# A decoder layer in three-pass fp32r matmuls: the first two feed-forward matrices reordered over ScalarE, GpSimd and VectorE, and the right end of memory moved by 128 bytes

## The reference, cut to what matters

```python
x = x + g1 * (concat(rms(o_sb), rms(o_dsa)) @ w_o)          # output projection
h = rms(x) * norm2_gain * (1 + sc2) + sh2                   # modulated norm
x = x + g2 * ((silu(h @ w_gate) * (h @ w_up)) @ w_down)     # feed-forward, width 2816
return rms(x) * final_gain * (1 + sc_f) + sh_f              # sc_f, sh_f from w_mod_final
```

## Time and profile before

| what | before |
|---|---|
| median of 3 runs | 1518.36 us (1517.19 to 1519.18) |
| the profiled execution | 1517.11 us |
| its span | 1515.4 us |
| TensorE busy | 1338.2 us, 88% |
| VectorE busy | 1078.7 us, 71% |
| ScalarE busy | 731.6 us, 48% |
| GpSimd busy | 732.5 us, 48% |
| TensorE's mean granted clock, share of full | 0.945 |
| chain that ended last: TensorE, VectorE | 42%, 5% |

### The profile page before, as it was taken

One profiled execution on the slowest core, in us unless ns is written; L12 is line 12 of the kernel. 1 busy time (PEld: TensorE's weight loads), 2 busy tenths in 40 slices (PEclk: granted clock), 3 DMA queues, 4 the chain that ended last, 5 costly groups with the idle time before them and its releaser, 6 DMA issues.

```text
span 1515.4 us, 18608 instructions
## 1 busy us (share of the span) xinstructions
PE 1338.2 (88%) x6085; PEld 1076.1 (71%) x6085; DVE 1078.7 (71%) x1582; ACT 731.6 (48%) x1262; POOL 732.5 (48%) x674
## 2 busy tenths in 40 slices
PE   1779999995877788876998889999999999999997
PEld 1657888774666566654776668888888888888786
DVE  4857599997777777755375987666666666577787
ACT  4436677734777778765222623322333333354332
POOL 1163444553445448877000235555555556587552
PEclk9799899996889899997799999999999999999999
DMA  9670234455343133320572225444444446889532
GB/s 337 185 210 16 83 119 145 139 181 132 74 95 78 47 98 100 89 68 24 222 227 103 87 84 183 143 155 160 159 150 149 154 160 204 296 303 333 182 112 111
DMA packets 124395, 223.35 MB, mean 147 GB/s; under 512 B 9450, under 2 KB 52564, under 8 KB 124052
## 3 DMA queue, kind: packets, MB, share of 16 engines
q1 hardware_dynamic: 124308, 222.27, 44.7%
HBM read 160.90 MB, written 57.93 MB: 144 GB/s over the span
## 4 chain that ended last, share of the span: by engine, by line
PE 42%; DVE 5%; issue 2%; ACT 1%; DMA 1%; POOL 0%; DVEq 0%; POOLq 0%; ACTq 0%; SPq 0%
PE ps_out L2150 26%; PE ps_out L2176 12%; PE ps_out L1492 2%; PE ps_out L1508 1%; DVE mod_acc_final L1575 1%; DMA scr_mod_final<-mod_acc_final 1%; PE ps_out L1862 0%; DVE y_gated L1605 0%; ACT square_junk L2070 0%; DVE x L2420 0%; DMA wgu_raw<-in_w_gate_dram 0%; DVE down_part L2418 0%; DVE y_full L1593 0%; DVE xhat L1874 0%; PE ps_out L1524 0%
## 5 line engine op out<-in xcount | busy, mean ns | idle before, releaser
L1849 POOL TENSOR_TENSOR wgu_lo<-wgu_raw,wgu_hi 128x512 fp32r<-128x512 f32 x64 | 91.5, 1436 | 147.3 <-ACT wgu_hi L1841 147.3
L2086 POOL TENSOR_TENSOR dn_lo<-dn_raw,dn_hi 128x512 fp32r<-128x512 f32 x77 | 127.3, 1671 | 67.2 <-ACT dn_hi L1994 67.1
L1841 ACT ACTIVATE wgu_hi<-wgu_sum 128x512 fp32r<-128x512 f32 x88 | 55.3, 632 | 201.9 <-DVE wgu_sum L2240 77.8
L2150 PE MATMUL ps_out<-h_b_t_hi,wgu_hi 128*128 128x512 f32 x352 | 140.4, 399 | 3.9 <-ACT p_part L1976 2.9
L2150 PE MATMUL ps_out<-h_b_t_hi,wgu_lo 128*128 128x512 f32 x352 | 139.8, 397 | 0.0
L2150 PE MATMUL ps_out<-h_b_t_lo,wgu_hi 128*128 128x512 f32 x352 | 139.7, 397 | 0.0
L1994 ACT ACTIVATE dn_hi<-dn_raw 128x1024 fp32r<-128x1024 f32 x77 | 81.2, 1062 | 114.7 <-PE ps_out L2176 57.1
L1148 POOL TENSOR_TENSOR a_rows<-beta,stick_left 128x1024 f32<-128x1024 f32 (+3 forms) x64 | 77.1, 1207 | 109.5 <-DVE stick_left L1196 109.5
L413 POOL TENSOR_TENSOR win_lo<-win_raw,win_hi 128x256 fp32r<-128x256 f32 (+1 forms) x84 | 62.3, 774 | 133.9 <-ACT win_hi L404 133.9
L2176 PE MATMUL ps_out<-dn_hi 128*128 128x512 f32 x308 | 120.4, 391 | 0.0
L2176 PE MATMUL ps_out<-dn_hi,dn_lo 128*128 128x512 f32 x308 | 120.1, 390 | 0.0
(11 more groups left out here) (327 smaller groups left out, 3827.0 us busy)
## 6 DMA issues: line engine op xcount, KB each, us to landing
scr_act_sums<-act_sums SPq DMA_DIRECT2D x11, 1792.0 KB, 6.8
dn_raw<-scr_act_sums SPq DMA_DIRECT2D x77, 256.0 KB, 5.2
wgu_raw<-in_w_gate_dram SPq DMA_DIRECT2D x11, 1024.0 KB, 5.4
wgu_raw<-in_w_up_dram SPq DMA_DIRECT2D x11, 1024.0 KB, 5.4
wd_sums<-in_w_down_dram SPq DMA_DIRECT2D x11, 1024.0 KB, 5.0
scr_wd_sums<-wd_sums SPq DMA_DIRECT2D x11, 1024.0 KB, 4.1
dn_raw<-scr_wd_sums SPq DMA_DIRECT2D x44, 256.0 KB, 7.0
win_raw<-in_w_in_dram SPq DMA_DIRECT2D x20, 512.0 KB, 4.5
```

Source lines behind the costliest of these rows:

```text
L1849: pool.tensor_tensor(sl[slot(m, x)][:], src, sh[slot(m, x)][:].bitcast(F32), ALU.subtract).then_inc(wlp, 1)
L2086: pool.tensor_tensor(bl[q % NSLOT][:, 1], braw[entry(q)][:, 1], bh[q % NSLOT][:, 1].bitcast(F32), ALU.subtract).then_inc(dlw, 1)
L2150: last = pe.matmul(bank(m, b), a[s][:, t], h[x][t // 2][:, t % 2], start=(fresh and t == 0 and a is sh and h is hh), stop=(t == 3 and a is ...
```

## The change

`xhat` is split in two: blocks 0 to 3 stay with VectorE (`early_xhat`) and come in front of step 8's work, not behind it; blocks 4 to 7 go to ScalarE (`late_xhat`). The transposes T0 to T7 take places one step or half a step later, the modulations and the splits with them. `late_rstd` of block 6 comes in front of GpSimd's first low parts. The six low parts of S3, S4 and A22 of the first two matrices go from VectorE to GpSimd. The hand-written orders of ScalarE and VectorE change. `mod_acc_final` goes from the left to the right, into the first 2 KB of a tile that the first modulated block overwrites, so the first `modulate` waits for all four stores of it. The pad on the right grows from 32 to 160 bytes.

```diff
-    fa = sbuf(nc, ctx, "mod_acc_final", [P, HALF])
+    fa = nc.alloc_sbuf_tensor_at("mod_acc_final", [P, HALF], F32, offset=g.top - 16 * 1024)
...
-    STEP_T = {(0, 9): 0, (1, 10): 1, (0, 10): 2, (1, 11): 3, (0, 11): 4, (1, 12): 5, (0, 12): 6, (0, 13): 7}
-    AFTER_COPY = {11: (0, 1), 12: (2, 3), 13: (4, 5), 14: (6,), 15: (7,)}
+    STEP_T = {(1, 10): 0, (0, 10): 1, (1, 11): 2, (0, 11): 3, (1, 12): 4, (0, 12): 5, (1, 13): 6, (0, 13): 7}
+    AFTER_COPY = {11: (0,), 12: (1, 2), 13: (3, 4), 14: (5, 6), 15: (7,)}
...
         then.first_highs(act)
+        for i in range(4, 7):
+            then.late_xhat(act, i)
         squares(NT - 1)
...
         late_rstd(4, 6, 2)
+        late_rstd(6, 7, 3)
         then.first_lows(pool, 0)
-        late_rstd(6, 7, 3)
         then.first_lows(pool, 1)
...
+            if n == 8:
+                for x in range(4):
+                    then.early_xhat(dve, x)
             dve.wait_ge(ysc, n + 1)
...
-            if n == 8:
-                for x in range(4):
-                    then.xhat(dve, x)
-            if n in (10, 11, 12):
-                then.split(dve, n - 10)
+            if n in (11, 12, 13):
+                then.split(dve, n - 11)
...
     def low_by_vector(self, m, x):
-        return x in LOW_DVE or (m < 2 and x in (P_S3, P_S4, P_A22))
+        return x in LOW_DVE
...
     def modulate(act, n):
+        if n == 0:
+            act.wait_ge(p4.fmo, 64)
...
-        pe.wait_ge(xhd, 4 + 4 * h)
+        pe.wait_ge(xha if h else xhd, 4)
...
+    def early_xhat(dve, i):
+        dve.wait_ge(p4.rs2, 1)
+        dve.wait_ge(x1_out[0], 16 * 4)
+        dve.tensor_scalar(g.x1[:, i], g.x1[:, i], g.rstd2[:, i:i + 1], None, ALU.mult).then_inc(xhd, 1)
+
+    def late_xhat(act, i):
+        act.wait_ge(p4.rs2, {4: 2, 5: 2, 6: 3, 7: 4}[i])
+        if i == 4:
+            act.wait_ge(p4.ybm, p4.NY)
+        act.activation(xh[i // 2 - 2][:, i % 2], g.x1[:, i], ACT.Copy, scale=g.rstd2[:, i:i + 1]).then_inc(xha, 1)
...
         def await_prepared(m):
             sp.wait_ge(wlp, lows_pool(m, P_A22))
-            if m < 2:
-                sp.wait_ge(wld, lows_dve(m, P_A22))
             sp.wait_ge(sums, sums_through(m, P_S4))
...
         act.wait_ge(p4.fmd, p4.NF)
         copy_p1(0)
         w_hi(act, 0, P_S1)
+        w_hi(act, 1, P_S1)
+        late_xhat(act, 7)
         copy_p1(1)
-        for n in range(KD, KD + 4):
-            modulate(act, n)
-        w_hi(act, 1, P_S1)
-        for n in range(KD + 4, 2 * KD):
+        for n in range(KD, 2 * KD):
             modulate(act, n)
         w_hi(act, 0, P_S2)
         w_hi(act, 1, P_S2)
+        t_hi(P_S2, t2, 2)
+        w_hi(act, 0, P_S3)
+        w_hi(act, 1, P_S3)
+        silu(0, 0)
+        w_hi(act, 0, P_S4)
+        w_hi(act, 1, P_S4)
+        t_hi(P_S3, f_t3, 4)
         act.wait_ge(hfr, 2 * KD)
         t_hi(P_S4, f_b22, 0)
-        w_hi(act, 0, P_S3)
-        w_hi(act, 1, P_S3)
-        t_hi(P_S2, t2, 2)
-        silu(0, 0)
-        t_hi(P_S3, f_t3, 4)
-        w_hi(act, 0, P_S4)
-        w_hi(act, 1, P_S4)
-        t_hi(P_A22, f_t4, 6)
         w_hi(act, 0, P_A22)
         w_hi(act, 1, P_A22)
+        t_hi(P_A22, f_t4, 6)
         w_hi(act, 2, P_A11)
         silu(0, 3)
         w_hi(act, 2, P_S1)
...
             pool.tensor_tensor(bl[q % NSLOT][:, 1], braw[entry(q)][:, 1], bh[q % NSLOT][:, 1].bitcast(F32),
                                ALU.subtract).then_inc(dlw, 1)
 
+        for x in (P_S3, P_S4, P_A22):
+            for m in range(2):
+                w_lo_pool(pool, m, x)
         for m in range(2, MATS):
             w_lo_pool(pool, m, P_A11)
             w_lo_pool(pool, m, P_A12)
...
             dve.tensor_tensor(bl[q % NSLOT][:, 0], braw[entry(q)][:, 0], bh[q % NSLOT][:, 0].bitcast(F32),
                               ALU.subtract).then_inc(dla, 1)
 
-        for i in range(4, 7):
-            xhat(dve, i)
         w_sum(0, P_S1)
-        xhat(dve, 7)
         w_sum(1, P_S1)
         split(dve, P_A12, f_t4, 1, 8, 4)
         w_sum(0, P_S2)
         w_sum(1, P_S2)
+        w_lo(0, P_S1)
+        w_lo(1, P_S1)
+        w_sum(0, P_S3)
         for pc in range(2):
             t_sum(t1, f_t3, f_b11, pc, full=KD + 2 * pc + 2)
         for pc in range(2):
             dve.wait_ge(tsm, pc + 1)
             dve.tensor_copy(hh[P_S1][pc][:], t1[pc][:]).then_inc(hid, 1)
-        w_lo(0, P_S1)
         for pc in range(2):
             dve.wait_ge(hid, 5 + pc)
             dve.tensor_tensor(hl[P_S1][pc][:], t1[pc][:], hh[P_S1][pc][:].bitcast(F32), ALU.subtract).then_inc(lod, 1)
-        w_lo(1, P_S1)
-        w_sum(0, P_S3)
         w_sum(1, P_S3)
         for pc in range(2):
             t_sum(t2, f_b22, t1, pc, full=KD + 4 + 2 * pc + 2, before=pc + 1)
         w_sum(0, P_S4)
+        w_lo(0, P_S2)
+        for pc in range(2):
+            t_lo(P_S2, t2, pc, 1 + pc)
+        w_sum(1, P_S4)
+        w_lo(1, P_S2)
         for pc in range(2):
             t_sum(f_t3, f_b22, f_t3, pc)
-        w_sum(1, P_S4)
         for pc in range(2):
-            t_lo(P_S2, t2, pc, 3 + pc)
-        w_lo(0, P_S2)
-        w_lo(1, P_S2)
-        for pc in range(2):
-            t_lo(P_S3, f_t3, pc, 5 + pc)
-        w_lo(0, P_S3)
-        w_lo(1, P_S3)
+            t_lo(P_S3, f_t3, pc, 3 + pc)
         first_act(0)
-        for pc in range(2):
-            t_lo(P_S4, f_b22, pc, 1 + pc)
         u2_of(0)
         u4_of(0)
-        w_lo(0, P_S4)
+        for pc in range(2):
+            t_lo(P_S4, f_b22, pc, 5 + pc)
+        u2_of(1)
+        u4_of(1)
         for pc in range(2):
             t_sum(f_t4, f_t4, t2, pc, before=3 + pc)
-        u2_of(1)
-        u4_of(1)
-        w_lo(1, P_S4)
         finish(0, 3)
         for pc in range(2):
             t_lo(P_A22, f_t4, pc, 7 + pc)
-        w_lo(0, P_A22)
-        w_lo(1, P_A22)
         w_sum(2, P_S1)
         finish(1, 3)
         finish(0, 1)
...
-            co.enter_context(nc.sbuf_tensor("right_pad", [P, 8], F32, side="right"))
+            co.enter_context(nc.sbuf_tensor("right_pad", [P, 40], F32, side="right"))
```

More of the change, by code:

```diff
@@ L1733, in phase5 @@
     raw_loaded = k.sems("wgu_loaded", 2)
-    xhd = k.sem("xhat2_ready")
+    xhd = k.sem("xhat2_dve_ready")
+    xha = k.sem("xhat2_act_ready")
     tr = k.sem("x1_transposed")
@@ L1863, in transposes @@
         m.then_inc(tr, 1)
-    def xhat(dve, i):
-        dve.wait_ge(p4.rs2, (1, 2, 3, 4)[max(0, i // 2 - 1) + (i == 7)])
-        if i < 4:
-            dve.wait_ge(x1_out[0], 16 * 4)
-            dst = g.x1[:, i]
-        else:
-            if i == 4:
-                dve.wait_ge(p4.ybm, p4.NY)
-            dst = xh[i // 2 - 2][:, i % 2]
-        dve.tensor_scalar(dst, g.x1[:, i], g.rstd2[:, i:i + 1], None, ALU.mult).then_inc(xhd, 1)
+    def early_xhat(dve, i):
[7 more added lines that the diff above has]
+        act.activation(xh[i // 2 - 2][:, i % 2], g.x1[:, i], ACT.Copy, scale=g.rstd2[:, i:i + 1]).then_inc(xha, 1)
     def split(dve, x, f, pc, full, at_):
@@ L1930, in sync @@
         sp.wait_ge(x1_out[1], 16 * (NT // 2))
-        sp.wait_ge(xhd, NT)
+        sp.wait_ge(xha, 4)
         load_wd(0)
@@ L1982, in silu @@
                 if m == 0:
-                    act.wait_ge(xhd, NT)
+                    act.wait_ge(xha, 4)
             else:
@@ L2290, in first_act @@
                 dve.wait_ge(x1_out[1], 16 * (NT // 2))
-                dve.wait_ge(xhd, NT)
+                dve.wait_ge(xha, 4)
             dve.tensor_tensor(acts[:, S_A11], bank(m, X), sg[:, 0], ALU.mult).then_inc(mulr, 1)
@@ L2505, in phase5 @@
     then.first_raw, then.spill, then.modulate, then.first_highs = first_raw, spill, modulate, first_highs
-    then.first_lows, then.transposes, then.xhat, then.split = first_lows, transposes, xhat, early_split
+    then.first_lows, then.transposes, then.split = first_lows, transposes, early_split
+    then.early_xhat, then.late_xhat = early_xhat, late_xhat
     return Programs(sync, scalar, gpsimd, tensor, vector)
```

## The result

The changed kernel takes 1502.15 us, median of four runs (1498.33 to 1503.82), beside 1517.78 for the kernel before with its fourth run (1512.39 to 1519.18). The ratio of the changed kernel's times to the other's is 0.9902, with a 95% interval of 0.9882 to 0.9923: 15 us faster (12 to 18). The profiled execution took 1503.75 us with a span of 1502.0.

The account below looks back on a forecast made before the run. TensorE was taken to bound from 907 us on, VectorE in front of it. Reordering 5.5 plus pad 6.5 made 12.0 off 1517.1, so 1505.1; the median lies 1.25 higher: forecast 1506.5, range 1500 to 1514.5.

Parts of the forecast that it names:

- The case named most likely: Whole kernel: reordering gains 5.5 us and the pad 6.5, 12.0 in sum; chance 0.50.
- Part 6, the pad: Matmuls of twenty matrices: the pad aligns `high` tiles with `low` weights, 6.0 us, with the output projection 6.5 taken.
- my slower rival: A11, S1, A12, S3: the new offset lengthens matmuls by 0.0066 us, 1520.2 us in all; slower side 0.09.
- the rival "worth nothing": All matrices: the pad gains nothing, only the reordering's 5.5 us remains, 1512.9 us; chance 0.24.
- Part 1, the seam at T0: Output projection: early `xhat` removes T0's 4.67 us wait, T1 waits 2.65; gain 2.5 us, less 1.2 to 1.75 if the clock falls.
- Part 2, the late `xhat` on ScalarE: Before T8: the fourth `xhat` ends at 848.5, T8 starts at 848.6 and not 851.65, 3.0 us earlier.
- Part 3, six low parts to GpSimd: First two matrices: VectorE gives up 3.6 us but is held 6.6, so it loses 3 us.
- Part 4, the load: Matrix 2's weights: SP issues the load at 877.3, not 888.6, and VectorE's 5.00 us wait goes.
- Part 5, the chain: VectorE from last x (844.5) to `w_sum(2, S1)`: 43.9 us, reached at 888.4; TensorE restarts at 901.3, 5.8 us earlier.
- The reordering: All parts but the pad, in front of TensorE's restart: 5.5 us gained, bounds 0 and 10.

Follow-up runs that it names:

- The last version: Changed kernel with only A22's two low parts on GpSimd, and TensorE's transposes and ScalarE's modulations moved in two tables of places: 1494.16 us, ratio 0.9875.

## Why the prediction was right, and where not

1506.5 us with a range of 1500.0 to 1514.5 was predicted, faster with 0.86; it is 1502.15 and faster, by 15 us where 12 were forecast. The case named most likely is the one that came: both halves of the change work, and they add. By steps:

*Part 6, the pad: right in kind, too small.* Put at 6.0 us over twenty matrices, measured 8.6, and 8.7 in the whole time by the run with the pad alone. The mis-sized term is S2, S3 and S4. I took 0.0025 us a matmul for S2 and let S3 and S4 keep what they had; all went to 0.2267, which is 0.07, 0.06 and 0.05 us a product in place of 0.03, 0 and 0. A11, S1, A12 and A22 gave what I had put for them. S3 I could have had from my own rule: both its h parts are `high`, and my slower rival counts it with those. S4's tiles all lie on the left, and no address of its own changed; so "each `high` tile gets the same place as the weights it meets" is not the full rule. That the pad alone, without the order, gives 8.7 us refutes the rival "worth nothing" (0.24). The Trainium skill, "SBUF — State Buffer", section "Who interferes with whom", says that TensorE never waits on anyone for SBUF. The prediction read a price of 0 for the pad out of it, and the runs go against that price. In this kernel a matmul's spacing depends on the distance between the two ends of memory; whether other engines have a part in it no run shows. The sum of the slower rival has a slip: 48 and 24 matmuls at its steps make 7.5 us and not 7.3, which changes nothing.

*Part 1, the seam at T0.* The times came as worked out: T1's gap 2.89 (2.65 expected), T4's 1.18 (1.2), T6's 2.02 (2.1), each released by ScalarE's modulation. The clock did fall behind T1 (at 815.4), and A11 starts at 842.41, 1.4 us before the old time, which is what the 2.5 us less a fall of 1.2 would give. But 1.4 is partly luck, as the two executions lost the clock differently further in front; where they lost it alike it was 0.7. The part that I credited with it, the early place of `xhat`, is worth nothing by the run with it undone; the loss at T1 eats it.

*Part 2, the late `xhat` on ScalarE: wrong.* The step that failed is "the fourth ends at 848.5, T8 starts at 848.6". The last x was to be there at 844.5; it came at 847.1. Three low parts in a row on GpSimd, 4.70 us, stand right beside steps 14 and 15 and hold VectorE by 2.3 us in all. From the last x to T8 it then took 4.7 us and not 4.1. T8 came at 851.78, not a bit earlier than before. A11 to T8 even grew from 7.8 to 9.4 us. The last version, in which those low parts hold nothing, has 7.9 again. What the late `xhat` is worth by itself is not shown: no run moves it back.

*Part 3, six low parts to GpSimd.* "VectorE loses 3 us": the sign is right, the size 1.7 to 2.7 (with six back) or 2.0 to 3.0 for four of them. The holds are in the trace (1.79 and 1.60 us for 0.69). The Trainium skill, "SBUF — State Buffer", section "Who interferes with whom", says that a VectorE instruction with two SBUF inputs and a GpSimd instruction that reads SBUF are in each other's way. The trace agrees, by these two rows.

*Part 4, the load.* Issued at 879.28 (877.3 expected), no wait of VectorE left. It is worth 4.8 to 5.8 us in the stage by the run with it late again, about the 5.00 of that wait.

*Part 5, the chain.* `w_sum(2, S1)` at 888.95 (888.4), restart at 902.58 (901.3). That it is this close is luck: VectorE's last x came 2.6 us later than I had it (847.1 and not 844.5), and from there to `w_sum(2, S1)` it took 41.9 us and not the 43.9 of my sum (41.9 to 42.9 in the other executions of the order). Part 3's runs explain 0.3 to 1.3 us of that: the six holds were put at 3.0 net and were 1.7 to 2.7. The rest is open. From `w_sum` to the restart I had "nothing changed" and 12.9 us; it took 13.6, since `w_sum` is now held by a low part on GpSimd (1.78 us for 0.69). Of TensorE's gaps on the way, put at 0.7, 1.9, 2.5, 2.9 and 1.3, there came 0.37, 3.49, 0.31, 2.77 and none. The reordering: 5.5 expected, 4.5 in front of the restart in the two profiles, and 3.3 (0.6 to 5.9) in the whole time by the run with the old pad.

So the sum hid two errors of opposite sign, 2.6 us too little for the pad and 1 to 2 too much for the order.

## What to carry to other kernels

When matmuls run back to back, divide the time of a product by its number and compare between products: a difference that comes back in every loop can be a property of where the tiles lie, and one pad that puts the two ends of memory at the right distance can pay for every matmul behind, even for a product whose own tiles don't move. Before moving work to an engine to relieve another, ask what the other reads: here six instructions on GpSimd cost VectorE more than they took off it, and they paid only because a load could start 9 us earlier, for which two of the six were enough. And a wait in TensorE's stream that ends with another engine's small instruction may be only that instruction's place in the queue: here two tables of places were worth some 4 us, as much as the whole reordering.

## What the runs showed of the hardware that I had not expected

The spacing of 512-column fp32r matmuls depends on the distance between the two ends of memory: 0.2267 us at 0, 256 and 512 bytes over the unit, 0.2300 on average at 64 (19.32 us for 84), 0.2318 at 128 (19.47 for 84). That it is the distance is shown by moving the left side in place of the right. Two things narrow it down. In A22 of the kernel before, whose high part of h lies on the left like the weights and whose low part on the right, only every third start is late:

```profile
997.70 0.39 PE L2150 MATMUL ps_out<-h_t_hi,wgu_hi 128*128 128x512 f32 x1
997.93 0.40 PE L2150 MATMUL ps_out<-h_t_lo,wgu_hi 128*128 128x512 f32 x1
998.16 0.39 PE L2150 MATMUL ps_out<-h_t_hi,wgu_lo 128*128 128x512 f32 x1
998.39 0.39 PE L2150 MATMUL ps_out<-h_t_hi,wgu_hi 128*128 128x512 f32 x1
```

In the mean of 18 matrices, behind the matmul that reads the right tile the next one starts after 0.234 us, behind the other two after 0.227 and 0.226. And in S4, all on the left and directly behind S3, the starts follow irregularly behind its first ten matmuls, after 0.224 to 0.236 us, and after 0.227 behind its last two; with 64 bytes of distance it has the same twelve numbers to 0.001 us. So S4 may carry over from the product in front of it what its own tiles don't cause; that is an argument and not shown. Against so simple a rule stands S2, which is made up like A22 and follows S1: it is late to its end (0.236, 0.234 and 0.230 behind its last three). Why a distance of 64 or 128 costs, and whether 32 or 192 do, is open. S4 takes 2.77 us for twelve in the run with the old pad and the new order too (988.07 to 990.84). That last run's two rows:

```profile
988.07 0.40 PE L2155 MATMUL ps_out<-h_b_hi,wgu_hi 128*128 128x512 f32 x1
...
990.84 0.39 PE L2155 MATMUL ps_out<-h_t_hi,wgu_hi 128*128 128x512 f32 x1
```

The granted clock of TensorE fell to the lower of its two levels at 815.4, 852.9 and 876.8, behind the gaps of 2.89, 3.49 and 2.77 us, in the changed kernel, and not behind those of 1.18, 2.02 and 2.10; but in the last version built here it fell at 828.6, behind the gap of 2.03 us at T7. T1's gap is 2.88 to 2.90 us long in seven executions, and in four of them the clock fell at it. So the same gap does not always bring a fall, and single executions differ by more than some of the parts measured here.
